# Neighbourhood attention: the next head pair's projection cut into sixteen like pieces, its transposes moved into the pair after

## The reference, cut to what matters

```python
q_l, k_l, v_l = jnp.split(h_lat @ w_qkv, 3, axis=-1)
q_c, k_c, v_c = jnp.split(h_ctx @ w_qkv, 3, axis=-1)
...
s_nb = jnp.einsum('bchd,bicjhd->bhcij', q_r, k_win).reshape(B, NA_HEADS, GRID_W, kh * NA_KW)
...
s_nb = s_nb + bias[None]
s_cx = jnp.einsum('bchd,blhd->bhcl', q_r, k_c)
p = jax.nn.softmax(jnp.concatenate([s_nb, s_cx], axis=-1).astype(jnp.float32), axis=-1).astype(v_l.dtype)
...
return jnp.einsum('bhcij,bicjhd->bchd', p_nb, v_win) + jnp.einsum('bhcl,blhd->bchd', p_cx, v_c)
```

## Time and profile before

| | |
|---|---|
| median of 3 runs | 4180.94 us (4176.02 to 4183.22) |
| profiled execution, its own time | 4184.53 us |
| its span, first to last instruction | 4182.5 us |
| busy over the span: PE, DVE, ACT, POOL | 3833.2, 1851.6, 1319.7, 459.4 us |
| first turn to last `values` of neighbourhood attention | about 1313 to 1631 us |

### The profile page before, as it was taken

One profiled execution on the slowest core, in us unless ns is written; L12 is line 12 of the kernel. 1 busy time (PEld: TensorE's weight loads), 2 busy tenths in 40 slices (PEclk: granted clock), 3 DMA queues, 4 the chain that ended last, 5 costly groups with the idle time before them and its releaser, 6 DMA issues.

```text
span 4182.5 us, 52761 instructions
## 1 busy us (share of the span) xinstructions
PE 3833.2 (92%) x21504; PEld 2995.4 (72%) x21504; DVE 1851.6 (44%) x2839; ACT 1319.7 (32%) x1950; POOL 459.4 (11%) x379
## 2 busy tenths in 40 slices
PE   7889989999997998999888898899998898889999
PEld 3555657888885887788766666688876666767887
DVE  3556544434334344444533455543333445554333
ACT  4334333313123333323324321232233433124222
POOL 1221201000012120000211220000021122000000
PEclk9999999999998999999999999999999999999999
DMA  5223421211211322222121210233222121113322
GB/s 195 83 90 111 127 95 43 70 61 61 68 49 61 106 71 91 81 95 97 57 55 38 79 46 26 67 93 100 91 67 60 33 75 46 31 50 100 101 91 71
DMA packets 327713, 317.04 MB, mean 76 GB/s; under 512 B 8944, under 2 KB 314000, under 8 KB 327344
## 3 DMA queue, kind: packets, MB, share of 16 engines
q1 hardware_dynamic: 327472, 313.68, 24.0%
HBM read 311.55 MB, written 2.10 MB: 75 GB/s over the span
## 4 chain that ended last, share of the span: by engine, by line
PE 80%; DVE 11%; ACT 4%; issue 2%; POOL 1%; DMA 1%; DVEq 0%; SPq 0%; ACTq 0%; POOLq 0%
PE PS L133 79%; DVE scr L147 5%; ACT scr L143 2%; DVE scr L157 1%; DVE scr L165 1%; DVE PS L161 1%; PE PS L136 1%; ACT L143 1%; DVE NBt L157 1%; DVE scr L169 1%; POOL ring_r L147 1%; DVE scr L177 0%; ACT NBt L143 0%; DVE scr L153 0%; POOL NBt L147 0%
## 5 line engine op out<-in xcount | busy, mean ns | idle before, releaser
L133 PE MATMUL PS<-scr 128*128 128x128 f32 (+7 forms) x7124 | 659.0, 284 | 124.8 <-DVE scr L147 65.0
L133 PEld LDWEIGHTS PS<-scr 128*128 128x128 f32 (+3 forms) x7124 | 512.8, 155 | 268.7 <-issue 103.2
L133 PE MATMUL PS<-ffn_h,ffn_w 128*128 128x512 f32 (+1 forms) x3168 | 616.1, 357 | 7.9 <-DVE ffn_h L157 5.7
L133 PEld LDWEIGHTS PS<-ffn_h,ffn_w 128*128 128x128 f32 x3168 | 524.6, 189 | 100.5 <-issue 9.1
L143 ACT ACTIVATE scr<-PS 128x256 f32<-128x256 f32 (+4 forms) x405 | 187.6, 463 | 740.7 <-PE PS L133 682.2
L133 PE MATMUL PS<-h_h,ring_r 128*128 128x512 f32 (+1 forms) x976 | 357.5, 429 | 38.5 <-POOL ring_r L147 24.6
L133 PE MATMUL PS<-mlp_h,mlp_w 128*128 128x512 f32 x1536 | 361.3, 396 | 0.0
L143 ACT ACTIVATE scr<-scr 128x256 f32<-128x256 f32 (+5 forms) x392 | 194.9, 497 | 524.7 <-DVE scr L157 322.4
L133 PE MATMUL PS<-mlp_g,mlp_w 128*128 128x512 f32 x1536 | 359.7, 396 | 0.0
L133 PEld LDWEIGHTS PS<-mlp_h,mlp_w 128*128 128x128 f32 x1536 | 288.4, 188 | 70.4 <-issue 1.0
L133 PEld LDWEIGHTS PS<-mlp_g,mlp_w 128*128 128x128 f32 x1536 | 288.5, 188 | 69.9
(11 more groups left out here) (153 smaller groups left out, 4739.6 us busy)
## 6 DMA issues: line engine op xcount, KB each, us to landing
ring<-in_ffn_w_in SPq DMA_DIRECT2D x44, 1024.0 KB, 5.0
scr<-in_ada_w SPq DMA_DIRECT2D x52, 768.0 KB, 4.8
ring<-in_w_up SPq DMA_DIRECT2D x32, 1024.0 KB, 5.5
ring<-in_w_down SPq DMA_DIRECT2D x32, 1024.0 KB, 5.3
ring<-in_w_in SPq DMA_DIRECT2D x60, 512.0 KB, 3.9
ring<-in_ffn_w_out SPq DMA_DIRECT2D x16, 1024.0 KB, 5.2
scr<-in_na_bias SPq DMA_DIRECT2D x32, 512.0 KB, 5.1
ring<-in_na_w_qkv SPq DMA_DIRECT2D x24, 512.0 KB, 4.1
```

What stands on the lines that cost most here:

```text
L133: return self.eng.matmul(o, lhsT=l, rhs=r, start=start, stop=stop) if self.eng else Nothing()
```

## The change

On PE the nine transposes of pair `tl` leave `project(tl)` and become `turned(tl)`, which runs in slot 0 of the pair after, in one block; for the last pair there is now a `project(8)` that holds only that. The products follow in the order q, latent keys, context keys, latent values, context values. q and the latent keys take four slots each with six matmuls in a slot (slots 1 to 8), the context keys two slots with twelve of 256 columns (9, 10), the latent values four slots (11 to 14) and the context values one slot with all 24 (15). ACT copies the transposes in slot 1, q in 5, the latent keys in 9, the context keys in 11, and both parts of the values in 15; it splits the next pair's q and k weights after slot 11's copy. POOL yields once more before its second split. SP's order is the same, written shorter.

```diff
-                bg = project(tl + 1) if tl < 7 else iter(())
+                bg = project(tl + 1)
...
-        def project(tl):
-            pe.wait_ge(*at("na_lo", "qk", tl))
-            yield from qk(tl, NQK[:2])
...
-            yield from qk(tl, NQK[2:])
+        def turned(tl):
+            pe.wait_ge(*at("na_made", "n_vt", tl, 1))
             for g in range(3):
                 o, before = cur["rg"].take("na_made", "n_vx", tl, g)
                 emptied(pe, before)
-                pe.wait_ge(*at("na_made", "n_vt", tl, 1))
                 for c in range(3):
                     v = V_AT[3 * g + c]
                     t = pe.tr(o[:, c * 128:c * 128 + 128], VT[:, v:v + 128], ident)
                 t.then_inc(*pe.up("na_in_full", "nvx_full", tl, g))
-                yield
-                yield
+
+        def project(tl):
+            if tl:
+                turned(tl - 1)
+                yield
+            if tl == 8:
+                return
+            pe.wait_ge(*at("na_lo", "qk", tl))
+            for (what, j, (t0, tn)), per in zip(NQK, (2, 2, 4)):
+                o_ = 0 if what == "q" else 1024
+                yield from product(tl, ("n_in", tl, j), ("n_full", tl, j), w8(o_, 1024), w8(2048 + o_, 1024), t0, tn, per)
+            pe.wait_ge(*at("na_lo", "v", tl))
+            for s, (t0, tn) in enumerate(LC):
+                yield from product(tl, ("n_vt", tl, s), ("nv_full", tl, s), w8(4096, 1024), w8(5120, 1024), t0, tn, (2, 8)[s])
...
         def project(tl):
-            u = tl % 2
-            split_act("v", tl)
...
+            if tl < 8:
+                split_act("v", tl)
+            if tl:
+                yield
+                for g in range(3):
+                    act.wait_ge(*at("na_in_full", "nvx_full", tl - 1, g))
+                    if tl >= 3:
+                        act.wait_ge(*at("no_full", 4 * (tl - 3) + 3))
+                    act.f(VX[(tl - 1) % 2][:, 3 * g:3 * g + 3, :], psum("na_made", "n_vx", tl - 1, g)[:, 0:384].rearrange("p (c e) -> p c e", c=3),
+                          ACT.Copy).then_inc(*act.up("na_made", "n_vx", tl - 1, g))
+            if tl == 8:
+                yield
+                return
+            for (what, j, (t0, tn)), n in zip(NQK, (4, 4, 2)):
+                yield from idles(n)
...
+            yield from idles(4)
+            values_in(tl, 0)
+            values_in(tl, 1)
+            yield
```

More of the change, by code:

```diff
@@ L1742, in project @@
             fetch()
-            for _ in range(6):
-                yield
+            yield from idles(6)
             fetch()
-            for _ in range(10):
-                yield
+            yield from idles(10)
         def scores(it):
@@ L1768, in three, with product @@
             return pe.mm(o, wl[:, k, :], nhh[:, k, c], False, k == 7)
[L1770 to L1783, removed]
-        def project(tl):
-            pe.wait_ge(*at("na_lo", "qk", tl))
-            yield from qk(tl, NQK[:2])
[L1788 to L1800, removed]
-            yield from qk(tl, NQK[2:])
+        def product(tl, name, full, wh, wl, t0, tn, per):
+            o, before = cur["rg"].take("na_made", *name)
+            emptied(pe, before)
+            for k in range(8):
+                pe.wait_ge(*at("nl", "na", k, int(t0 == 0)))
+                t = three(o[:, 0:tn], wh, wl, slice(t0, t0 + tn), k)
+                if k == 7:
+                    t.then_inc(*pe.up("na_in_full", *full))
+                if k % per == per - 1:
+                    yield
+        def turned(tl):
+            pe.wait_ge(*at("na_made", "n_vt", tl, 1))
             for g in range(3):
@@ L1862, in na_act @@
         norm_act(act, "na", LC, ada_gain(1, 0, f_col)[1], na_parts)
[L1864 to L1871, removed]
@@ L1873, in project, with values_in @@
-        def project(tl):
-            u = tl % 2
-            split_act("v", tl)
-            for what, j, (t0, tn) in NQK[:2]:
-                yield from qk(tl, what, j, t0, tn)
-            for s, (t0, tn) in enumerate(LC):
-                yield
[L1880 to L1883, removed]
-                yield
-            what, j, (t0, tn) = NQK[2]
-            yield from qk(tl, what, j, t0, tn)
+        def values_in(tl, s):
+            t0, tn = LC[s]
+            act.wait_ge(*at("na_in_full", "nv_full", tl, s))
+            if tl:
+                act.wait_ge(*at("na_in_full", "nvx_full", tl - 1, 2))
+            act.f(VT[:, t0:t0 + tn], psum("na_made", "n_vt", tl, s)[:, 0:tn], ACT.Copy).then_inc(*act.up("na_made", "n_vt", tl, s))
@@ new lines, in project @@
+        def project(tl):
+            if tl < 8:
+                split_act("v", tl)
+            if tl:
+                yield
+                for g in range(3):
[5 more added lines that the diff above has]
+            if tl == 8:
+                yield
+                return
+            for (what, j, (t0, tn)), n in zip(NQK, (4, 4, 2)):
+                yield from idles(n)
+                act.wait_ge(*at("na_in_full", "n_full", tl, j))
+                if tl >= 2:
+                    act.wait_ge(*at("ns_full", 4 * (tl - 2) + 3))
+                act.f(QT[tl % 2] if what == "q" else KTt[tl % 2][:, t0:t0 + tn], psum("na_made", "n_in", tl, j)[:, 0:tn], ACT.Copy,
+                      scale=64 ** -0.5 if what == "q" else 1.0).then_inc(*act.up("na_made", "n_in", tl, j))
@@ L1965, in project @@
         def project(tl):
+            if tl == 8:
+                return
             split_pool("v", tl)
-            for _ in range(10):
-                yield
+            yield from idles(11)
             if tl < 7:
                 split_pool("qk", tl + 1)
-            for _ in range(6):
-                yield
+            yield from idles(5)
         na_turns(project, idle, idle, idle, idle)
```

## The result

The changed kernel takes 4209.89 us, median of 6 runs (4207.24 to 4220.75), against 4176.03 us before (6 runs, 4169.66 to 4183.22). The ratio is 1.0085, 95% interval 1.0069 to 1.010; the two medians alone give 1.0081, some 34 us slower. That is the side that the prediction gave, and the time lies within its range of 4208 to 4217 us.

The account below looks back on a forecast made before the run. PE was taken to set the pace; 1.3 us up to pair 1, six pairs of 2.4 + 2.3 and 1.9 in pair 7 make +31.4 us, 4212 us against the median 4180.9. Range 4208 to 4217; 8 in 10: 4195 to 4223.

Parts of the forecast that it names:

- The wait: First turn of a pair: q waits for the first transposes' bank, beginning 7.5 us behind the turn's start; PE pauses 4.3 us.
- The other turns: Second, third and fourth turns of a pair: 9.54, 9.69 and 11.06 us, with the waits for DVE's copies gone.
- The clock: Behind the first-turn pause in each of pairs 0 to 6, a lower granted clock loses 2.3 us, bounds 0 and 3.0.
- Rival 1: First turns: the pause comes but the clock does not fall behind it; +15 us, 4196 us; chance 0.14.
- Sum: Whole stage: 1.3 + 6 x (2.4 + 2.3) + 1.9 = +31.4 us, forecast 4212 us.
- up to pair 1: Stage's start and pair 0: first `scores` 2.6 us sooner, yet pair 1 begins 1.3 us later with pause and clock loss.
- pairs 1 to 6: Six pairs, each 2.4 us longer by its turns and 2.3 us more by the lower clock.
- pair 7: Last pair's first turn: `values` needs all three transpose copies, PE through at 7.6 us against 5.78 before; +1.9 us.
- Rival 3: First turn: q does not wait, so the even spread pays as a whole; about -16 us, 4165 us; chance 0.05.
- Rival 4: Each turn's 2.0 us for `flip` and starts hides 0.5 us waiting, removed; clock holds; +3 us, 4184 us; chance 0.06.

## Why the prediction was right

**The wait.** The prediction put q 7.5 us behind the turn's start and the pause at 4.3 us. Measured: 7.61 and 4.32 (from pair 2 on; 7.60 and 4.30 in pair 1). That it is the bank of T0, the first group, and that bank alone, is shown by the kernel that copies one group ahead; that its place behind the exponentials and the split makes it late, by the copies ahead and by the split behind (1.15 us less for a split of 1.06 us).

**The other turns.** 9.54, 9.69 and 11.06 us were worked out; 9.55, 9.71 and 11.06 are there. The prices taken from the earlier trace rows carry over because nothing in these turns waits.

**The clock.** Taken: 2.3 us in each of seven pauses, from the four in the earlier trace rows. Measured in the first turns of pairs 1 to 6, against 13.6 us at a full clock: 1.4, 2.6, 1.6, 2.7, 1.6 and 2.7, mean 2.1. In pair 0, where the pause is 7.52 us long, it is 2.3. The loss alternates; the 7 us behind two successive pauses of equal length have 0.62 and 0.77. That it is the pause, and that it accounts for nearly half of the result, is shown by the two kernels with filled pauses. Rival 1 leaned on the 3.20 us pause of the earlier trace rows as a case in which the clock holds. That was one case: behind pauses of 3.17 us it fell six times of six, behind 2.53 us five of six. The trace before already had a pause hardly longer than 3.20 us with a large loss, which the prediction doesn't weigh:

```profile
2427.90:2431.44 3.54, 0.00 (x0) 0.00 (x0) 3.40 (x5) 3.20 (x5) 0.00 (x0) 0.87 0.53 148
2431.44:2438.44 7.00, 7.00 (x18) 5.36 (x18) 6.62 (x7) 1.06 (x1) 4.41 (x3) 0.58 0.00 0
```

A single row was no bound; the rival's 0.14 was, if anything, too much.

**Sum.** To compare the two executions in the stage itself, I measure from the stage's first weight split on ACT, which stands ahead of everything that was changed, to the last `values` on PE. After:

```profile
1254.89 1.91 ACT L143 ACTIVATE na_w<-ring 128x2048 fp32r<-128x2048 f32 x1
...
1655.36 1.09 PE L133 MATMUL PS<-scr 128*64 128x128 f32 x16 [0.78 <-DVE scr L165]
```

Before, the same two stand at 1262.02 and 1629.86. From start to start, the stage took 400.5 us against 367.8: +32.6, against +31.4 in the prediction. By its terms: up to pair 1 +2.1 (predicted +1.3), pairs 1 to 6 +27.3 (28.2), pair 7 +3.2 (1.9). The sum is closer than its terms, since their errors partly cancel.

The first was mis-sized by 0.8 us: the first `scores` began 1.5 us sooner than before and not 2.6. The products ahead of it ended 48.9 us behind the first weight split and not 47.6 as before, with a granted clock of 0.50 instead of 0.57 in the 13.9 us of them in which the last parts of `h` come in.

Pair 7 was mis-sized most. Its first turn took 7.62 us, as worked out (7.6, which against 5.78 before is +1.8 and not +1.9), but behind that turn's wait of 2.55 us the clock was down too, and the second turn took 7.13 us instead of 5.71:

```profile
1637.46 5.65 PE L133 MATMUL PS<-scr 128*64 128x128 f32 x40 [2.55 <-ACT scr L143]
```

The 40 matmuls took 5.65 us; in the earlier trace rows the same group took 4.26. The prediction counted seven pauses, in the pairs 0 to 6, and put the clock at nothing in pair 7; but PE's `values`, `scores` and `flip` lie in the chain there. That the clock falls behind this wait is not certain either: with the flip in the pause, pair 7 had the same wait, and its 40 matmuls took 4.26 us at a clock of 1.00.

The spans of the two profiled executions differ by less, 22.6 us. The stage's first split came 7.1 us sooner in the one after, though nothing ahead of it had changed, and the rest of the program behind the stage took 2.9 us less. I take both for spread between executions; the medians differ by 34 us.

**Rival 3** (no wait, 4165 us) is not what happened, but it is the price of the thing undone: it stood for 16 us less than the kernel before, and the kernel with the copies ahead takes 15.8 us less. **Rival 4** would need waits hidden in the 2.0 us of each turn that like slots remove; the later turns have the lengths worked out with that 2.0, so like slots removed none.

## What to carry to other kernels

When producers rotate over a small ring of banks, a piece of work that is moved takes the copy that frees its bank along, and on the copying engine that copy may land behind a chain that starts only now: look who takes the bank next, and how late the copy is in the queue of the other engine. Moving the copy, not the matmuls, was the whole difference here (+34 us to -16 us). And price a pause of PE by what it costs in clock behind it as well: here 2.1 us on top of a pause of 4.3 us, which nearly doubled what the change lost, and most pauses of 2.5 us still cost 1.6.

## What was not expected of the hardware

Float32 transposes hold the clock: 4.5 us of them in a row and a wait of 1.04 us behind, and the granted clock stayed 1.00.

The clock falls late and unevenly: behind the 3.17 us pauses, PE ran at full speed for some 0.8 to 1.4 us before the lower level came; behind pauses of 4.3 us the loss was 1.4 us in one pair and 2.6 us in the next; behind 2.53 us it was 1.6 us or nothing. Even a wait of 1.94 us, in pair 7 of the kernel with the first copy ahead, had a lower clock behind it (40 matmuls in 5.77 us); one of 2.55 us, in pair 7 of the kernel with the flip in the pause, had 1.00 behind it. So length alone does not decide; what does stays open.
